# First block's attention: one unit of work is a pair of heads instead of one head

## What is computed

```python
def softmax_with_sink(s, sink_hg):
    sk = jnp.broadcast_to(sink_hg.astype(jnp.float32)[:, :, None, None], s.shape[:-1] + (1,))
    p = jax.nn.softmax(jnp.concatenate([s, sk], axis=-1), axis=-1)
    return p[..., :-1]
```

## Time and profile before

| | |
|---|---|
| median of 3 runs | 2284.94 us (2282.61 to 2288.09) |
| profiled execution: its time | 2283.03 us |
| its span on the trace | 2281.6 us |
| PE busy | 2058.5 us (90%), mean granted clock 0.944 |
| DVE, ACT, POOL busy | 952.3, 876.6, 664.2 us (42, 38, 29%) |
| chain that ended last | PE 74%, DVE 15%, ACT 5% |
| L904 logits, 96 units | PE 94.1 us |
| L928 values, 96 units | PE 83.8 us |

### The profile page before, as it was taken

The page is one execution under the profiler, slowest core; times in us unless marked ns, Lnnn a source line. Parts: engine busy times, 40 slices in busy tenths (PEclk is TensorE's granted clock), DMA queues, the critical chain, the costliest instruction groups (busy, mean ns, idle before and its releaser), DMA issues.

```text
span 2281.6 us, 30554 instructions
## 1 busy us (share of the span) xinstructions
PE 2058.5 (90%) x12588; PEld 1709.6 (75%) x12588; DVE 952.3 (42%) x1716; ACT 876.6 (38%) x1488; POOL 664.2 (29%) x297
## 2 busy tenths in 40 slices
PE   4899999998999999889988997988987889899786
PEld 1565667676788888677778997977877788778686
DVE  2424322364111111435455445467334645843555
ACT  1212333352321222334454443455452444644432
POOL 1221111233444444231123442423232333222322
PEclk7899999999999999989998998999998999999988
DMA  7423444521222322232224564533332444243231
GB/s 267 162 74 139 140 146 177 212 74 65 93 93 84 110 93 86 76 107 75 65 84 145 181 203 147 167 111 120 102 102 79 135 148 148 76 134 105 93 100 58
DMA packets 76554, 272.26 MB, mean 119 GB/s; under 512 B 8192, under 2 KB 11392, under 8 KB 76416
## 3 DMA queue, kind: packets, MB, share of 16 engines
q1 hardware_dynamic: 72576, 264.27, 34.5%
q10 hardware_dynamic: 3840, 6.04, 0.7%
HBM read 269.23 MB, written 1.05 MB: 118 GB/s over the span
## 4 chain that ended last, share of the span: by engine, by line
PE 74%; DVE 15%; ACT 5%; issue 2%; DMA 2%; POOL 2%; ACTq 0%; DVEq 0%; POOLq 0%
PE bank L745 20%; PE bank L746 18%; PE bank L747 18%; PE bank L904 4%; PE bank L928 3%; DVE low L1507 2%; PE bank L826 2%; PE bank L915 2%; DVE xc L1554 2%; ACT high L1141 2%; PE bank L867 1%; DMA xc<-ctx_in 1%; PE bank L893 1%; PE bank L838 1%; POOL few L1458 1%
## 5 line engine op out<-in xcount | busy, mean ns | idle before, releaser
L1449 POOL TENSOR_TENSOR low<-raw,high 128x1024 fp32r<-128x1024 f32 x260 | 627.3, 2415 | 1418.1 <-ACT high L1141 1418.1
L745 PE MATMUL bank<-h,high 128*128 128x256 f32 (+1 forms) x2432 | 807.5, 332 | 58.4 <-DVE h L1646 12.7
L746 PE MATMUL bank<-h,high 128*128 128x256 f32 (+1 forms) x2432 | 766.4, 315 | 0.0
L747 PE MATMUL bank<-h,low 128*128 128x256 f32 (+1 forms) x2432 | 765.5, 315 | 0.0
L745 PEld LDWEIGHTS bank<-h,high 128*128 128x128 f32 x2432 | 473.0, 195 | 158.4 <-issue 60.3
L746 PEld LDWEIGHTS bank<-h,high 128*128 128x128 f32 x2432 | 474.3, 195 | 29.6 <-issue 2.4
L747 PEld LDWEIGHTS bank<-h,low 128*128 128x128 f32 x2432 | 472.8, 194 | 29.7
L1141 ACT ACTIVATE high<-raw 128x1024 fp32r<-128x1024 f32 x408 | 426.8, 1051 | 145.8 <-PE bank L747 118.3
L1507 DVE TENSOR_TENSOR low<-raw,high 128x1024 fp32r<-128x1024 f32 x148 | 198.8, 1343 | 223.1 <-ACT high L1141 222.9
L1261 ACT ACTIVATE prob<-bank,small 128x512 f32<-128x512 f32 (+1 forms) x96 | 59.2, 617 | 187.4 <-DVE small L1690 111.2
L745 PE MATMUL bank<-hid,high 128*128 128x512 f32 (+1 forms) x352 | 118.2, 336 | 0.0
(11 more groups left out here) (262 smaller groups left out, 2671.9 us busy)
## 6 DMA issues: line engine op xcount, KB each, us to landing
raw<-stream SPq DMA_DIRECT2D x504, 512.0 KB, 3.4
xc<-x_in ACTq DMA_DIRECT2D x1, 1024.0 KB, 17.1
xc<-ctx_in ACTq DMA_DIRECT2D x1, 1024.0 KB, 28.5
out<-xc ACTq DMA_DIRECT2D x1, 1024.0 KB, 4.8
cst<-consts ACTq DMA_DIRECT2D x1, 960.0 KB, 29.0
cst<-consts ACTq DMA_DIRECT2D x1, 704.0 KB, 22.5
ukw<-uk ACTq DMA_DIRECT2D x1, 512.0 KB, 3.3
uvw<-uv ACTq DMA_DIRECT2D x1, 512.0 KB, 4.2
```

The costliest lines, as they stand in the source:

```text
L745: mm(dst, wh, xh, start=start, stop=False)
L746: mm(dst, wh, xl, start=False, stop=False)
L747: return mm(dst, wl, xh, start=False, stop=stop)
L1449: tt(low[:, i % PAIRS, :], raw[:, slot % SLOTS, :], high[:, i % PAIRS, :].bitcast(F32), ALU.subtract).then_inc(S["lo_pool"], 1)
```

## The change

A unit of the loop becomes a pair of heads (b, t, j), heads j and j + 4, which lie in the two halves (g = 0, 1; partitions 0-63, 64-127) of one tile of Q. There are 48 pairs instead of 96 heads.

- `S` issues both halves' logits in a row, into two banks. `masked_max` and exp are per head; for b = 0 the minimum with the sink, the sink's difference and its exp are one small instruction each per pair, and exp waits for them.
- a new step `even`: DVE adds the sink's term, takes the reciprocal of two sums and divides both heads' probabilities in SBUF, ahead of the transposes.
- `turn` transposes both heads into two banks; ACT copies the first, DVE the second.
- `PV`: the values (64 columns) are stationary, the transposed probabilities move; the halves write partitions 0-63 and 64-127 of bank 7. Outputs come out already transposed.
- `finish` and the transposes of `deliver` go; `deliver` is two copies each on ACT and DVE from bank 7 to Q.
- The loop has 8 blocks in one round: 3, then `even` and `turn` of the pair before, 3, `PV` of the pair before, 2.

```diff
-        units = [(b, t, h) for t in range(n // P) for b in range(2) for h in range(NH)]
-        per = 4
-        pending = []
-        for i in range(len(units) + 4):
-            if i < len(units):
-                o.step("S", l, i, *units[i])
-            o.fill(per)
-            if pending and i % 8 == 5:
-                o.step("deliver", l, *pending.pop(0))
-            if 2 <= i < len(units) + 2:
-                o.step("turn", l, i - 2, *units[i - 2])
-            if 3 <= i < len(units) + 3:
-                b, t, h = units[i - 3]
-                o.step("PV", l, i - 3, b, t, h)
-                if h == NH - 1:
-                    o.step("finish", l, b, t)
-                    pending.append((b, t))
-        while pending:
-            o.step("deliver", l, *pending.pop(0))
+        pairs = [(b, t, j) for t in range(n // P) for b in range(2) for j in range(4)]
+        for i in range(len(pairs) + 1):
+            if i < len(pairs):
+                o.step("S", l, i, *pairs[i])
+            o.fill(3)
+            if i < len(pairs):
+                o.step("even", l, i, *pairs[i])
+            if i:
+                o.step("turn", l, i - 1, *pairs[i - 1])
+            o.fill(3)
+            if i:
+                b, t, j = pairs[i - 1]
+                o.step("PV", l, i - 1, b, t, j)
+                if j == 3:
+                    o.step("deliver", l, b, t)
+            o.fill(2)
...
-        elif kind in ("S", "score", "latent", "read", "centre"):
+        elif kind == "S":
+            bank[s] = (turn("lgt"), turn("lgt"))
+        elif kind == "turn":
+            bank[s] = (turn("trp"), turn("trp"))
+        elif kind in ("score", "latent", "read", "centre"):
...
-            prob[l] = [sb(f"prob{l}_{i}", [P, 512], scope=attn) for i in range(3)]
+            prob[l] = [*(sb(f"prob{l}_{i}", [P, 512], scope=attn) for i in range(3)), tmp[0]]
...
+        def out_of(l, b, t, g, odd):
+            src = banks[7].rearrange("p (i o t) -> p o i t", o=2, t=P)[head(g), odd, :, :]
+            return src, Q[l][head(odd), 4 * b + 2 * g:4 * b + 2 * g + 2, t * P:(t + 1) * P]
+        def stat(l, i):
+            return small[:, 8 * (i % 4):8 * (i % 4) + 8]
...
+                    keys, w = keys_of(t)
+                    pe.wait_ge("rope", no["rope", "Q", l, 4 * b_ + j])
+                    for g, b in enumerate(bank_of[step]):
+                        if b in freed:
+                            pe.wait_ge(*freed[b])
+                        mm(banks[b][:, 0:w], Q[l][head(g), 4 * b_ + j, t * P:(t + 1) * P], K[l][head(g), b_, keys],
+                           start=True, stop=True).then_inc(S["S"], 1)
+                        freed[b] = ("exp", 2 * no[step] - 1 + g)
+                    _, w = keys_of(t)
+                    for g, b in enumerate(bank_of[step]):
+                        p = prob[l][2 * (i % 2) + g]
+                        if b in freed:
+                            pe.wait_ge(*freed[b])
+                        pe.wait_ge("even", 2 * no[step] - 1 + g)
+                        for s in range(w // P):
+                            ins = nc.tensor.transpose(banks[b][:, s * P:(s + 1) * P], p[:, s * P:(s + 1) * P], ident)
+                        ins.then_inc(S["turn"], 1)
+                        freed[b] = ("turned_dve" if g else "turned_act", no[step])
+                elif kind == "PV":
+                    keys, w = keys_of(t)
+                    first = (ALLT - w) // P
+                    if j == 0 and 7 in freed:
+                        pe.wait_ge(*freed[7])
+                        if freed[7][0] == "delivered_dve":
+                            pe.wait_ge("delivered_act", freed[7][1])
+                    pe.wait_ge(*drained["V", l, 3])
+                    pe.wait_ge("turned_act", no[step])
+                    pe.wait_ge("turned_dve", no[step])
+                        for g in range(2):
+                            c = P * b_ + HD * g
+                            ins = mm(banks[7][head(g), j * P:(j + 1) * P], V[l][:, first + s, c:c + HD],
+                                     probT[l][g][:, s * P:(s + 1) * P], start=s == 0, stop=s == w // P - 1)
+                            if s == w // P - 1:
+                                ins.then_inc(S["PV"], 1)
+                    if j == 3:
+                        freed[7] = ("delivered_dve", no["deliver", l, b_, t])
...
+                    (_, w), st, at = keys_of(t), stat(l, i), 2 * no[step] - 1
+                    act.wait_ge("rope", no["rope", "Q", l, 7])
+                    for g, b in enumerate(bank_of[step]):
+                        if i >= 2:
+                            act.wait_ge("turn", at + g - 4)
+                        if b_ == 0:
+                            act.wait_ge("sink_max", sinks[l, i])
+                        else:
+                            act.wait_ge("masked_max", at + g)
+                        do(prob[l][2 * (i % 2) + g][:, 0:w], banks[b][:, 0:w], ACTF.Exp, bias=st[:, g:g + 1],
+                           accum_out=st[:, 2 + g:3 + g]).then_inc(S["exp"], 1)
+                        act.wait_ge("sunk", sinks[l, i])
+                        do(st[:, 4:6], st[:, 4:6], ACTF.Exp).then_inc(S["sunk_exp"], 1)
                 elif kind == "turn":
+                    act.wait_ge("turn", 2 * no[step] - 1)
+                    if i:
+                        act.wait_ge("PV", 2 * no[step] - 2)
+                    do(probT[l][0][:, 0:w], banks[bank_of[step][0]][:, 0:w], ACTF.Copy).then_inc(S["turned_act"], 1)
                 elif kind == "deliver":
+                    act.wait_ge("PV", 8 * no[step])
+                    for odd in range(2):
+                        src, dst = out_of(l, b_, t, 0, odd)
+                        ins = do(dst, src, ACTF.Copy)
+                    ins.then_inc(S["delivered_act"], 1)
...
+                    (_, w), st, at = keys_of(t), stat(l, i), 2 * no[step] - 1
+                    for g, b in enumerate(bank_of[step]):
+                        ps = banks[b]
+                        dve.wait_ge("S", at + g)
+                        if b_ == 0 and t < 2:
+                            o = slice((1 - t) * P, (2 - t) * P)
+                            tt(ps[:, o], ps[:, o], const("window", t * P, t * P + P), ALU.add).then_inc(S["dve_own"], 1)
+                            dve.wait_ge("dve_own", own)
+                        if no[step] > 4:
+                            dve.wait_ge("even", at + g - 8)
+                        nc.vector.tensor_reduce(st[:, g:g + 1], ps[:, 0:w], AX.X, ALU.max,
+                                                negate=True).then_inc(S["masked_max"], 1)
+                    if b_ == 0:
+                        at_sink = 8 * l + j
+                        of_sink = slice(at_sink, at_sink + 5, 4)
+                        dve.wait_ge("nsink", 1)
+                        dve.wait_ge("masked_max", at + 1)
+                        tt(st[:, 0:2], st[:, 0:2], small_sink[:, of_sink], ALU.min).then_inc(S["sink_max"], 1)
+                        dve.wait_ge("sink_max", sinks[l, i])
+                        tt(st[:, 4:6], st[:, 0:2], small_sink[:, of_sink], ALU.subtract).then_inc(S["sunk"], 1)
+                elif kind == "even":
+                    (_, w), st, at = keys_of(t), stat(l, i), 2 * no[step] - 1
+                    dve.wait_ge("exp", at + 1)
+                    if b_ == 0:
+                        dve.wait_ge("sunk_exp", sinks[l, i])
+                        tt(st[:, 2:4], st[:, 2:4], st[:, 4:6], ALU.add).then_inc(S["dve_own"], 1)
+                    nc.vector.reciprocal(st[:, 6:8], st[:, 2:4]).then_inc(S["dve_own"], 1)
+                    dve.wait_ge("dve_own", own)
+                    for g in range(2):
+                        p = prob[l][2 * (i % 2) + g][:, 0:w]
+                        ts(p, p, st[:, 6 + g:7 + g], None, ALU.mult).then_inc(S["even"], 1)
                 elif kind == "turn":
+                    dve.wait_ge("turn", 2 * no[step])
+                    if i:
+                        dve.wait_ge("PV", 2 * no[step] - 2)
+                    nc.vector.tensor_copy(probT[l][1][:, 0:w], banks[bank_of[step][1]][:, 0:w]).then_inc(S["turned_dve"], 1)
+                elif kind == "deliver":
+                    dve.wait_ge("PV", 8 * no[step])
+                    for odd in range(2):
+                        src, dst = out_of(l, b_, t, 1, odd)
+                        ins = nc.vector.tensor_copy(dst, src)
+                    ins.then_inc(S["delivered_dve"], 1)
```

More of the change, by code:

```diff
@@ L505, in psum_banks @@
             bank[s] = (turn("lgt"), turn("lgt"))
[L506 removed]
+        elif kind in ("adac", "rope", "totok", "absorb", "turn2", "blend", "gcol"):
             bank[s] = turn("trp")
@@ L539 @@
 rope_pe rope_sin rope
-S masked_max sink_max exp turn turned_act turned_dve PV sunk sunk_exp finish deliver delivered
+S masked_max sink_max sunk exp sunk_exp even turn turned_act turned_dve PV delivered_act delivered_dve
 hm_hi hm sig mixed mix_hi mix hid_hi hid
@@ L595, in build @@
```

(26 more changed lines are left out.)

116 lines of the change are left out of this document (12 added, 104 removed).

## The result

The changed kernel takes 2344.43 us (median of 4 runs, 2339.48 to 2349.59) where the kernel before takes 2286.28 beside it: ratio 1.0259, interval 1.0235 to 1.0283. It is 58 us slower. Forecast were 2320 and 2294 to 2346, so the sign and the mechanism held and the size was 24 us short. The time lies only 1.6 us inside the upper end of the range, and above the 2306 to 2335 that had more than half of the chance.

A forecast was written before the change was run, and what follows sets the result against it. PE was taken to bound the kernel before; after, the softmax chain inside a round, except beside first-layer gates. 2283.03 + 17 at full clock + 20 for the lowered clock = 2320 us, range 2294 to 2346.

The forecast's parts named there:

- PE's side: Both loops, 512 keys: a pair's logits 1.05 us instead of 2.1, values 1.0 against 2 x 0.93; ada batch of three 1.0.
- rival 1: Both loops: softmax covered after all, PE bounds the rounds; about -30 us in each layer, 2220; chance 0.05.
- The new wait: At the values, PE waits for DVE's copy behind the whole softmax; 6.9 us after logits start (512 keys, window).
- POOL's hold on the minimum: Second layer, rounds where POOL makes `low`: the sink's minimum, due at 3.15, comes at 3.9: +0.6 us.
- The delay by DVE's `low`: Second layer, every second round: `low` precedes the maxima on DVE and moves them from 1.16 to 2.6: +1.44 us.
- +17 at full clock: Both loops together, before any price for a lower clock: second layer +14.5 us, first layer +2.6.
- A: Case of pairs with window and sink; second-layer round 9.7 us against 7.8 before, seven full rounds: +13.
- B: Case of pairs without window and sink; values can start at 5.1 us (512 keys); second-layer round 7.7 against 7.8.
- the start: First layer's loop: first round, without `PV` and `turn`, some 5.1 us shorter than a full one: -1.5 us.
- the clock's term: Both loops: 18 pauses of 3 us or more lower PE's clock; 0 to 2.8 us each, 1.1 taken: +20.
- Rival 3: Clock stays low through the rounds with pauses, B rounds suffer too: +17 + 50 to 60 us, 2346; chance 0.13.
- half of the possible price: B rounds, divisions beside POOL: 0.6 us of 0 to 1.2 (256 keys), 0.24 (512 keys), 0.15 (second layer).

The follow-up runs named there:

- the deep order: Changed kernel with one more round: values two rounds behind logits, transposes last in the round, four buffers of transposed probabilities: 2240.43 us, ratio 0.9813.
- the filled start: The deep order with eight blocks put ahead of the second pair's logits: 2232.85 us, ratio 0.9761.
- Eight blocks ahead: Changed kernel with eight blocks put ahead of the second pair's logits in each layer: 2344.63 us, ratio 1.0254.
- the filled pauses: Changed kernel with 18 unused products added ahead of the values' wait, in second-layer window rounds and first-layer window rounds with ada: 2339.73 us, ratio 1.0246.
- four, four and none: Changed kernel with a round's eight blocks as 4, 4 and none behind PV, instead of 3, 3, 2: 2307.19 us, ratio 1.0115.
- four and four: The deep order with a round's blocks as 4 and 4 instead of 3, 3, 2: 2246.37 us, ratio 0.9825; run again unchanged 2251.64.

## Why the prediction was right, and where it was short

**PE's side: right.** A pair's logits 1.13 us, values 1.09 (`240.05` below), an ada batch of three 1.06. What rival 1 worked out for PE alone was -60 us; the deep order shows -54, with the filled start -59.

```profile
240.05 1.09 PE L936 MATMUL bank<-probT,V 128*64 128x128 f32 x16 [1.39 <-DVE probT L1714]
```

**The new wait: right in place, order and length.** DVE's copy releases PE at the values, 77.1 us in all. Forecast from logits to values 6.9 us and 0.6 for POOL's hold on the minimum; measured 7.6. The delay by DVE's `low` was 2.6 us as forecast. The forecast of +17 at full clock holds some 77 us of pauses against those 60 us of work; measured are 81. Two steps of the working are off by less than 0.1 us: its own terms give 3.41 and not 3.35 for the start of exp, and 4.91 behind it and not 4.95.

**Rounds** (forecast in brackets): first layer, 512 keys, window: ada 10.7 to 11.6 (9.8), gates 9.85 to 10.8 (9.7); without: 7.53 and 9.85 (7.4 and 9.7). 256 keys, A: 7.0 to 8.4 (7.9) and 8.54 to 8.7 (8.4); B 6.55 (6.15) and 8.54 (8.4), but the last ada round 9.83. Second layer, A: 11.34 in the mean (9.7 and 1.1 for the clock); B 8.73 (7.7). The full clock lengths come out where nothing lowers the clock; what is over is in rounds with the long pauses.

**The first step that failed: the start.** It was put at -1.5 us (4.65 and 9.7 for the first two rounds of the first layer, from the step order alone). It took 2.91 and 19.54, so +8.1 instead. In the second layer, for whose start the sum has no term, it took 3.99 and 15.59 against some 5.0 and 9.7 by the same count, +4.9. The fourth head's logits need the bank of the first head. Before, twelve blocks stood ahead of them; now it is eight, and the bank is held by an exp that waits for the rotation on DVE, which the profile of before showed, and for the table load, which there was hidden. In the first layer's two rounds PE is idle for 4.28 us, all of it this wait, and works at a mean clock of 0.77, which makes the rest; in the second layer the bank wait is 2.02. Together 13 of the 22 us that the loops took over the forecast (59.6 against 17 + 20), a part of them also counted under the clock below. Eight blocks ahead took some 7 of the 13 back in these rounds, and in the deep order the whole kernel gained 8: that shows the wait as the larger part.

**The second: the size of the clock's term.** Eighteen pauses at 1.1 us made 20 us. The table above has 33, part of them in the two starts, and the filled pauses show at least 11.8 on the path. The bounds of the prediction (0 to 2.8 a pause) held, except in the kernel with four, four and none, where one pause cost 3.1 in the next round. How much of the 33 lies on the path is known only between those two numbers. Rounds with DVE's `low` were counted as +1.44 without a share of the clock; there 1.66 instead of 0.84 was measured as the difference. Rival 3, clock low throughout, stands at 2346 in the prediction, but its own terms (+17 and +50 to 60) give 2350 to 2360. The range reached the measured time only because it was drawn up to that 2346, and that is luck. The rival's reason is not what happened: the clock went up and down within each round (1.13 us for logits in one, 2.08 in the next).

**POOL beside DVE.** By the row of before a small operation with two inputs is held to POOL's end; the divisions got half of the possible price. A row of the changed kernel shows the division held in full:

```profile
380.98 2.36 POOL L1444 TENSOR_TENSOR low<-raw,high 128x1024 fp32r<-128x1024 f32 x1 [13.18 <-ACT high L1138]
...
382.05 1.71 DVE L1706 TENSOR_SCALAR prob<-prob,small 128x256 f32<-128x256 f32 x2
```

Two divisions of 256 columns take 1.71 us instead of some 0.6: the first ends with POOL (383.34) and the second right behind it (383.76). The Trainium skill (GPSIMD Engine Reference, Key points) says that POOL shares its SBUF interfaces with DVE instructions that have two SBUF inputs or run in a 2-port mode; the divisions read one tensor in SBUF, so this row bears on the second half as the earlier trace rows did on the first. What it cost in the changed kernel can be read from the means of the divisions by form. Those that write `tmp` come second in their pair and were never held:

```profile
L1706 DVE TENSOR_SCALAR prob<-prob,small 128x512 f32<-128x512 f32 x48 | 22.9, 505 | 1.1
...
L1706 DVE TENSOR_SCALAR prob<-prob,small 128x256 f32<-128x256 f32 x24 | 14.2, 619 | 0.6
...
L1706 DVE TENSOR_SCALAR tmp<-tmp,small 128x512 f32<-128x512 f32 x16 | 7.7, 480 | 0.0
...
L1706 DVE TENSOR_SCALAR tmp<-tmp,small 128x256 f32<-128x256 f32 x8 | 2.8, 348 | 0.0
```

48 x 0.025 and 24 x 0.271 us are 7.7 us, by this estimate, of which the prediction had about half. 3.2 of them fall into one round, the last ada round of the first layer, where POOL makes four `low` in a row, two divisions take 3.80 us and PE waits 3.81: that is the 9.83 above, a case that the sum has no term for.

## What to carry to other kernels

- Fewer instructions on the engine that bounds are worth nothing if the change also takes the slack out of the chain beside it. Count the rounds between producer and consumer for every engine's program order: here the same 54 us saved on PE gave +58 or, with the copy one step earlier, -8, and with one more round and a filled start -55.
- A pause of PE of 3 us and more, as here, is paid twice, in itself and in the work behind it at half clock (behind the 1.39 us of the row at 240.05 it stayed full); the second part is largest if that work is bound by PE. Removing a wait then gives more than its length.
- Work moved into a pause gains only if the place that it leaves gets shorter too.
- A fixed cost such as a table load is free ahead of a wait and on the path behind it: look for it at the start of a stage whose first activation frees a bank.

## What the runs showed that was not expected

The same products have two paces at the same granted clock. In the second layer's large products behind the loops, PE is busy without a break at clock 1.00, but in 30 us it gets through 267 or through 257 records. The deep order, then its version with four and four, that kernel again, the deep order with the filled start, and the one with PE kept busy:

```profile
1220.00:1250.00 30.00, 30.00 (x267) 30.00 (x266) 10.87 (x16) 13.31 (x20) 13.86 (x6) 1.00 0.59 194
```

```profile
1220.00:1250.00 30.00, 30.00 (x257) 30.00 (x257) 11.64 (x17) 14.04 (x21) 11.95 (x5) 1.00 0.57 186
```

```profile
1220.00:1250.00 30.00, 30.00 (x258) 30.00 (x257) 11.15 (x17) 14.87 (x22) 12.94 (x6) 1.00 0.54 178
```

```profile
1220.00:1250.00 30.00, 30.00 (x257) 30.00 (x256) 11.47 (x15) 11.65 (x14) 11.99 (x5) 1.00 0.55 176
```

```profile
1280.00:1310.00 30.00, 30.00 (x257) 30.00 (x256) 11.53 (x16) 14.35 (x22) 12.01 (x5) 1.00 0.58 192
```

From the end of the second loop to the end of the kernel it makes 1134 to 1138 us instead of 1125 to 1131 in the other kernels, about 8. The two executions of one program, taken at different times, show the same pace, so it seems to belong to the program and not to the execution. The work in this stretch is the same in all of them; only the instructions ahead of it differ in number or order. What sets it stays open; it was not tried. For this case it means that the fastest version might run some 7 us faster at the other pace, which no run shows, and that differences under 10 us between these kernels can't be put down to their edits by the time alone: the loops' lengths have to be compared.
